# First and third attention: both heads of a pair multiplied at once in the two halves of the rows

## The reference, cut to what matters

```python
# A: 16 heads of 64, 4 key heads; a window of 3 blocks of 128 keys and all 256 context keys
s_loc = jnp.einsum('bqhgd,bkhd->bhgqk', qs, ks).astype(jnp.float32) * scale
s_ctx = jnp.einsum('bqhgd,bkhd->bhgqk', qs, kc).astype(jnp.float32) * scale
p = jax.nn.softmax(jnp.concatenate([s_loc, s_ctx, sink], axis=-1), axis=-1).astype(dt)
# and the 256 context queries against the 256 context keys, with the same heads
s = jnp.einsum('bqhgd,bkhd->bhgqk', qc, kc).astype(jnp.float32) * scale
# E: 8 heads of 64, 2 key heads; a chunk of 64 queries reads its own and 2 earlier chunks
s = jnp.einsum('bqhgd,bjhd->bhgqj', q_c, k_c).astype(F32) * scale
```

## Time and profile before

| | us |
|---|---|
| three runs | 2131.64, 2136.08, 2538.79 (median 2136.08) |
| the profiled execution | 2130.91 |
| its span | 2129.0 |
| PE busy in the span | 2009.5 (94%) |
| DVE busy | 997.8 (47%) |
| ACT busy | 882.3 (41%) |
| POOL busy | 698.8 (33%) |

### The profile page before, as it was taken

One profiled execution on the slowest core, in us unless ns is written; L12 is line 12 of the kernel. 1 busy time (PEld: TensorE's weight loads), 2 busy tenths in 40 slices (PEclk: granted clock), 3 DMA queues, 4 the chain that ended last, 5 costly groups with the idle time before them and its releaser, 6 DMA issues.

```text
span 2129.0 us, 28194 instructions
## 1 busy us (share of the span) xinstructions
PE 2009.5 (94%) x10600; PEld 1569.0 (74%) x10600; DVE 997.8 (47%) x1774; ACT 882.3 (41%) x1668; POOL 698.8 (33%) x394
## 2 busy tenths in 40 slices
PE   5999999999999999998899999999998899999998
PEld 3888655688665567887677888887885477888886
DVE  3520778523376653378436435343116625525254
ACT  4322667423376654535553222235225643323233
POOL 1322122342100045331234444443442334444433
PEclk9999999999999999998899999999999999999999
DMA  8222333132100013231124433332332122333332
GB/s 297 60 67 63 100 100 109 51 106 59 44 1 1 1 30 88 62 97 33 40 82 149 135 95 89 105 92 75 109 97 60 45 78 80 109 98 93 100 92 85
DMA packets 209467, 174.36 MB, mean 82 GB/s; under 512 B 6080, under 2 KB 180775, under 8 KB 208183
## 3 DMA queue, kind: packets, MB, share of 16 engines
q1 hardware_dynamic: 206096, 163.86, 25.4%
q0 software_dynamic: 2192, 8.45, 1.2%
q10 hardware_dynamic: 1047, 0.26, 0.1%
HBM read 170.41 MB, written 7.38 MB: 84 GB/s over the span
## 4 chain that ended last, share of the span: by engine, by line
PE 43%; issue 4%; ACT 2%; DVE 2%; POOL 2%; POOLq 0%; DVEq 0%; ACTq 0%
PE ps L369 13%; PE ps L371 13%; PE ps L370 13%; PE ps L737 1%; POOL WL L1563 1%; PE ps L701 1%; PE ps L599 1%; ACT PB L653 0%; ACT TMP L514 0%; PE ps L682 0%; DVE PB L641 0%; PE ps L618 0%; DVE XC L2549 0%; PE ps L448 0%; POOL YT L1551 0%
## 5 line engine op out<-in xcount | busy, mean ns | idle before, releaser
L1563 POOL TENSOR_TENSOR WL<-raww,WH 128x1024 fp32r<-128x1024 f32 (+1 forms) x247 | 583.2, 2366 | 910.1 <-ACT WH L321 901.1
L369 PE MATMUL ps<-HH,WH 128*128 128x512 f32 (+1 forms) x1368 | 523.2, 382 | 16.5 <-DVE HL L2529 7.8
L370 PE MATMUL ps<-HL,WH 128*128 128x512 f32 (+1 forms) x1368 | 519.1, 379 | 0.0
L371 PE MATMUL ps<-HH,WL 128*128 128x512 f32 (+1 forms) x1368 | 518.5, 379 | 0.0
L321 ACT ACTIVATE WH<-raww 128x1024 fp32r<-128x1024 f32 (+1 forms) x247 | 254.7, 1036 | 412.1 <-PE ps L371 408.8
L369 PEld LDWEIGHTS ps<-HH,WH 128*128 128x128 f32 x1368 | 259.6, 190 | 73.8 <-issue 17.8
L371 PEld LDWEIGHTS ps<-HH,WL 128*128 128x128 f32 x1368 | 259.6, 190 | 48.5
L370 PEld LDWEIGHTS ps<-HL,WH 128*128 128x128 f32 x1368 | 260.0, 190 | 46.7
L701 PE MATMUL ps<-ident,PB 128*128 128x128 f32 x952 | 157.5, 283 | 24.5 <-ACT PB L653 16.0
L653 ACT ACTIVATE PB<-PB,NB 128x512 f32<-128x512 f32 (+3 forms) x192 | 116.5, 607 | 72.7 <-DVE NB L641 69.8
L701 PEld LDWEIGHTS ps<-ident,PB 128*128 128x128 f32 x952 | 109.5, 142 | 50.2 <-ACT PB L653 26.9
(11 more groups left out here) (346 smaller groups left out, 3113.4 us busy)
## 6 DMA issues: line engine op xcount, KB each, us to landing
raww<-in_ffn_w_up SPq DMA_DIRECT2D x88, 512.0 KB, 3.8
raww<-in_ffn_w_down SPq DMA_DIRECT2D x40, 512.0 KB, 3.3
raww<-in_ada_w SPq DMA_DIRECT2D x32, 512.0 KB, 3.6
raww<-in_odd_w_in SPq DMA_DIRECT2D x24, 512.0 KB, 3.8
raww<-in_a_w_in SPq DMA_DIRECT2D x20, 512.0 KB, 3.8
raww<-in_even_w_in SPq DMA_DIRECT2D x17, 512.0 KB, 3.9
ADA<-in_ada_w SPq DMA_DIRECT2D x6, 1024.0 KB, 16.5
raww<-in_b_w_in SPq DMA_DIRECT2D x12, 512.0 KB, 3.8
```

Source lines behind the costliest of these rows:

```text
L369: nc.tensor.matmul(out, lh, rh, start=start and k == ks[0], stop=False)
L370: nc.tensor.matmul(out, lh, rl, start=False, stop=False)
L371: ins = nc.tensor.matmul(out, ll, rh, start=False, stop=stop and k == ks[-1])
L1563: nc.gpsimd.tensor_tensor(lo, raw_slot(k), hi.bitcast(F32), ALU.subtract).then_inc(*split_lo.mark(k))
```

## The change

A and E become paired as O is. For each `m` the order is now tile 0 of head 0, tile 0 of head 1, tile 1 of head 0, and so on, and `pair_scores` makes both tiles' scores in the even steps. It waits for the banks of both tiles before its first product. In E each tile has one bank of four (`single`); in A each has two, so a pair has all four. A tile's scores are three products of 64 rows instead of two of 128, and the two heads' products stand in turn. q high and q low of both heads are now made by one instruction each over all 128 rows (`both_q_high`, `both_q_low`), and earlier: in A in steps 2 and 3 of a block, and in E likewise. In the ctx tiles of A and in E, which of DVE and ACT copies the transposed probabilities alternates with i + hh instead of i. E uses other buffers for the probabilities (4 instead of 3), one of which shares memory with WL, so POOL waits for `pv_made["E", 5]` before it splits the weights that come next. For O only the helper's form changes.

```diff
         def pair_scores(pe, A, r, i):
-            w = A["jobs"][r]["tiles"][i]["n"] * P
+            if "score_wait" in A:
+                A["score_wait"](pe, r, i)
+            todo = []
             for h in (r, r + 1):
-                claim(pe, A["at"](h, i) % 4, (max_made, (A["name"], h, i)))
-            A["score_wait"](pe, r, i)
-            for n, (q, k) in enumerate(A["products"](r)):
-                for h in (r, r + 1):
-                    p0 = HD * (h % 2)
-                    ins = nc.tensor.matmul(ps[:, A["at"](h, i) % 4, 0:w], q[p0:p0 + HD, i * P:(i + 1) * P], k[p0:p0 + HD, 0:w],
-                                           start=(n == 0), stop=(n == 2), tile_position=(p0, 0))
-                    if n == 2:
-                        ins.then_inc(*scores_made.mark(A["name"], h, i))
+                t, tl = A["at"](h, i), A["jobs"][h]["tiles"][i]
+                first = t % 4 if A.get("single") else 2 * (t % 2)
+                spans = sorted({(tl["off"] + c0) // 512 for c0, _, _, _ in tl["parts"]})
+                for b in spans:
+                    claim(pe, first + b, (max_made, (A["name"], h, i)))
+                todo.append([(first + (tl["off"] + c0) // 512, (tl["off"] + c0) % 512, w, q, k) for c0, w, q, k in tl["parts"]])
+            for n in range(len(todo[0])):
+                for h in range(2):
+                    b, c, w, q, k = todo[h][n]
+                    same = [x for x in range(len(todo[h])) if todo[h][x][0] == b]
+                    ins = nc.tensor.matmul(ps[:, b, c:c + w], q, k, start=(n == same[0]), stop=(n == same[-1]),
+                                           skip_group_check=True, tile_position=(HD * h, 0))
+                    if n == len(todo[0]) - 1:
+                        ins.then_inc(*scores_made.mark(A["name"], r + h, i))
...
+        def both_q_high(act, A, m):
+            if m >= 2:
+                n = A["per"] * (m - 1) - 1
+                act.wait_ge(*scores_made[A["name"], n, A["jobs"][n]["nq"] - 1])
+            nc.scalar.activation(A["q2"][m % 2][:, 0, :], A["q"][:, m, :], ACT.Copy).then_inc(*act_out.mark("q2", A["name"], m))
+
+        def both_q_low(dve, A, m):
+            dve.wait_ge(*act_out["q2", A["name"], m])
+            nc.vector.tensor_tensor(A["q2"][m % 2][:, 1, :], A["q"][:, m, :], A["q2"][m % 2][:, 0, :].bitcast(F32),
+                                    ALU.subtract).then_inc(*dve_out.mark("q2", A["name"], m))
...
-                                q = a_q2[m % 2][:, hh, i * P:(i + 1) * P]
+                                qh, ql = (a_q2[m % 2][p0:p0 + HD, j, i * P:(i + 1) * P] for j in range(2))
                                 lo, hi = max(i - 1, 0), min(i + 2, NT)
                                 nl = hi - lo
-                                parts = [(0, C, q, k[:, S:R]) for k in (kh, kl)]
-                                parts += [(2 * P, nl * P, q, k[:, lo * P:hi * P]) for k in (kh, kl)]
+                                parts = [(c0, w, q, k[p0:p0 + HD, a:a + w]) for q, k in ((qh, kh), (ql, kh), (qh, kl))
+                                         for c0, w, a in ((0, C, S), (2 * P, nl * P, lo * P))]
...
-                                      "fill_pe": a_fill_pe, "fill_dve": a_fill_dve, "per": 4, "gate": a_gate,
+                                      "fill_pe": a_fill_pe, "fill_dve": a_fill_dve, "per": 4, "paired": True, "gate": a_gate,
...
-                                      "per": 2, "pt": lambda r: ((0, 1, 3)[(r + 1) % 3], 0), "bc": BC, "bc_free": lambda r: o_made["E", (r // 2, "lat")], "q": e_q, "k": e_k, "q2": e_q2, "kh": e_kh, "kl": e_kl}))
+                                      "per": 2, "paired": True, "single": True,
+                                      "pt": lambda r: ((4, 2, 5, 6)[r % 4], 0), "pt_free": lambda r: (r - 4) | 1, "bc": BC, "bc_free": lambda r: o_made["E", (r // 2, "lat")], "q": e_q, "k": e_k, "q2": e_q2, "kh": e_kh, "kl": e_kl}))
...
             split_low(pool, ("e_q", 3))
+            pool.wait_ge(*pv_made["E", 5])
             split_low(pool, ("o_q", 7))
```

More of the change, by code:

```diff
@@ L882, in finish_att @@
             if A.get("paired"):
-                A["seq"] = [(r + h, i) for r in range(0, len(jobs), 2) for i in range(NT) for h in range(2)]
+                A["seq"] = [(r + h, i) for r in range(0, len(jobs), 2) for i in range(jobs[r]["nq"]) for h in range(2)]
             else:
@@ L1007, in a_jobs @@
                             for i in range(2):
-                                q = a_q2[m % 2][:, hh, S + i * P:S + (i + 1) * P]
-                                tiles.append(tile(2, [(0, C, q, k[:, S:R]) for k in (kh, kl)], [(0, [4, 5], ("dve", "act")[i])],
+                                qh, ql = (a_q2[m % 2][p0:p0 + HD, j, S + i * P:S + (i + 1) * P] for j in range(2))
+                                tiles.append(tile(2, [(0, C, q, k[p0:p0 + HD, S:R]) for q, k in ((qh, kh), (ql, kh), (qh, kl))],
+                                                  [(0, [4, 5], ("dve", "act")[(i + hh) % 2])],
                                                   0, masks[:, 0:C]))
@@ L1324, in e_jobs @@
                     for i in range(NT):
-                        q = e_q2[m % 2][:, hh, i * P:(i + 1) * P]
                         lo = max(i - 1, 0)
                         nl = i + 1 - lo
-                        parts = [(0, nl * P, q, k[:, lo * P:(i + 1) * P]) for k in (e_kh[kv], e_kl[:, kv, :])]
-                        tiles.append(tile(nl, parts, [(0, list(range(lo, i + 1)), ("dve", "act")[i % 2])],
+                        qh, ql = (e_q2[m % 2][p0:p0 + HD, j, i * P:(i + 1) * P] for j in range(2))
+                        kh, kl = (k[p0:p0 + HD, lo * P:(i + 1) * P] for k in (e_kh[kv], e_kl[:, kv, :]))
+                        tiles.append(tile(nl, [(0, nl * P, q, k) for q, k in ((qh, kh), (ql, kh), (qh, kl))],
+                                          [(0, list(range(lo, i + 1)), ("dve", "act")[(i + hh) % 2])],
                                           0, masks[:, (7 - nl) * P:7 * P]))
@@ L1375, in o_jobs @@
                     w = (i + 1) * P
-                    tiles.append(tile(i + 1, None, [(0, list(range(i + 1)), ("dve", "act")[(i + m) % 2])],
+                    qh, ql, kh, kl = (b[m // 2 % 2][p0:p0 + HD, :] for b in (o_qh, o_ql, o_kh, o_kl))
+                    parts = [(0, w, q[:, i * P:(i + 1) * P], k[:, 0:w]) for q, k in ((qh, kh), (ql, kh), (qh, kl))]
+                    tiles.append(tile(i + 1, parts, [(0, list(range(i + 1)), ("dve", "act")[(i + m) % 2])],
                                       0, o_band[:, m % 4, 512 - w:512]))
```

69 lines of the change are left out of this document (27 added, 42 removed).

## The result

| | before | after |
|---|---|---|
| median of 14 runs, us | 2133.85 | 2138.65 |
| the profiled execution | 2130.91 | 2139.68 |
| A, between the linear products around it | 183.9 | 192.4 |
| E, likewise | 55.7 | 55.6 |
| O, likewise | 93.4 | 96.1 |

The ratio is 1.0027 with a 95% interval of 1.0019 to 1.0036: slower by 0.3%, under the 2% called slower here, but clear of noise. One of the 14 runs of before lies at 2538.79 and is left out of the ratio. The number (2138.65) is inside the range of 2113 to 2145; the sign is not the forecast one: I had 2129 against 2131.9 in my own sum (and 2136 as the median of the three runs then known).

What follows compares the result with a forecast made beforehand. PE, 94% busy, was taken to bound A before the change; in E engines wait for each other. The profiled 2130.9 + 4 (A) - 6.5 (E) + 1 (undisturbed runs) gave 2129 us, range 2113 to 2145.

Steps and rivals of the forecast that it cites:

- What the scores cost: PE in A: paired rounds 0.12 or 0.17 us apart, 17 us less issue time, 2 us returned by switches.
- The walk of a block and its multiplication: A: one block walked, 23.2 against 22.4 us; five blocks +0.9, three -0.3, plus 0.5 for waits: +4 us.
- My own sign: A: each pair's first score within 0.1 us of the second maximum's end in steps 2 to 8.
- the second failed step: E: 8 tiles in 9.2 us, by O's ratio 1.17; three pairs gain 2.0 each, the first 0.6: -6.5 us.
- the sign of being wrong that I had set: The forecast is wrong if A is under 176 us or E's tiles keep their 11 us.
- The sum: Whole kernel: 2130.9 + 4 for A - 6.5 for E + 1 for undisturbed runs = 2129 us.
- Rival 2: A's coupling costs more, each hand-over late, 0.35 us in each of 48 pairs: A +17, E -4, 2145; chance 0.17.
- Rival 1: PE's saved time in A comes through: A -9, E -8, whole 2115 us; chance 0.20.
- Rival 3: The clock falls in A, to 0.95: +4 or 5 us, 2134; chance 0.18 together with Rival 4.
- Rival 4: E gets no faster, bound by ACT's exponentials or the half clock: 2134 us; chance 0.18 together with Rival 3.
- my own case: Whole kernel: A +4 and E -6.5 us give 2129, own range 2122 to 2136; chance 0.42.
- Rival 5: The row halves don't overlap: 17 x 2 more us on PE, 2155; chance 0.03.

Runs made afterwards that it cites:

- swap_a: Changed kernel, but in A's step 2 ACT copies the spread out of its bank before making q high; A 191.2 us, median 2138.83, ratio 1.0028 to before.
- late_e: Changed kernel, but in E DVE's output work of an even step comes behind the pair's second maximum; E 48.7 us, median 2135.00, ratio 1.0008 to before.
- seq_a: Changed kernel, but in A a pair's score products are issued head after head instead of in turn; A 203.0 us, median 2150.68, ratio 1.0083 to before.
- late_a: Changed kernel, but in A DVE's even-step work other than maximum and copy comes behind the second maximum; A 192.1 us, median 2143.00, ratio 1.0040 to before.
- banks_a: Changed kernel, but A's tiles with 2 and 4 key blocks take one score bank each; A 187.5 us, median 2134.55, ratio 1.0010 to before.
- e_coupled: Changed kernel, but in E a pair's scores wait for both maxima of the pair before; E 56.5 us, median 2145.57, ratio 1.0062 to before.

## Why the prediction was wrong

1. **What the scores cost: right.** The rounds stand 0.12 and 0.17 apart, the groups of scores lost 14.7 us together (55.3 to 40.6), forecast 17 less 2 for the switches. That PE's saved time would then come through in steps 0, 1 and 4, 5 did not hold (item 2). The switches are in the records: from the last score to a transpose 0.21 instead of 0.12 (256 columns) and 0.27 instead of 0.18 (384); from a transpose to a score never under 0.20, where the old form had 0.03. That is 0.26 for in and out together, where I took 0.1 to 0.2 each. Behind a product with the values or a filler the scores start after 0.31 in both forms, so there the way in costs nothing more.
2. **The walk of a block and its multiplication: the kind right, the term short. First failed step.** A was forecast 4 us longer and got 8.5 longer. In the block that I walked each lat step is within 0.35 of the forecast, and it got 1.3 longer for 0.8. The loss where the maxima bind was sized well: 1.0 and 0.8 a block in steps 2, 3 and 6, 7 would be 14.4 in all, and 13.4 was measured. What failed is the rest:
   - The gains of the PE-bound steps did not come. The walk has 0.4 and 0.3 a block less in steps 0, 1 and 4, 5, which would be 5.6; measured was 0.6.
   - The hand-over from the second maximum to the next scores was put at 0.02 us and is 0.25 (319.04 to 319.29) ahead of steps 4 and 6 where the maximum binds, and 0.15 ahead of step 8. That is 0.6 of the 0.8 by which the walked block exceeds 22.9. My own sign, first scores within 0.1 of the maximum's end, was not met.
   - One block stood for all. The three that prepare keys (1, 3, 5) were to get 0.9 shorter together, from a length of 24.1 read in one of them, and got 1.5 longer: block 1 had lasted 23.0 (238.39 to 261.36) and lasted 24.3. Block 0 had lasted 18.5 and lasted 20.6, 1.2 of it in steps 0, 1 (1.83 to 3.00). The five others together got 6.2 longer for 4.5.
   - The first pair of the stage waits for all four banks, 0.8.

   Fillers in steps 2 and 3 are not among the missing parts, though swap_a gains 0.6 in three such steps: the old form had paid for them too (3.63 with one, 2.76 without, in the same steps). There are 32 fillers, not 28.
3. **E: the second failed step.** I took 1.17 of the fullest engine's work from O and put it on E, 2.0 us for each of three pairs of heads alike and 0.6 for the first. Nothing in E was walked. The first gained 1.6, the second 1.2, the third some 0.5 and the fourth nothing, 2.8 in the mean (56.8 of two profiles to 54.0 of nine), not 6.5; the third's 14.0 in the changed kernel is the sign of being wrong that I had set (tiles that keep their 11 us). In E three instructions of DVE, 1.8 us, stand between two maxima of a pair: the same pattern that I had priced in A, at three times its size, and late_e shows that they bind. With that order mended E gained 7 to 8 in all, near my 6.5, but not as I had it: the second and third pairs of heads take 10.2 and 10.5 for my 9.2, and 3 us come in the last eight tiles (20.7 to 17.4). That nearness is in part luck.
4. **The sum.** -6.5 became -2.8 and +4 became +8.5. From the median of the undisturbed runs of before (2133.49, where I had 2131.9) this gives 2139.2, and 2138.65 was measured. Two terms of opposite sign, each off by about 4 us in the same direction, turned a forecast of 2.5 less into 5 to 6 more; with either one alone put right the forecast would have been a small loss.
5. **The rivals.** Rival 2 (coupling costs more, E -4, 2145) was the nearest and had 0.17; it decides from a lat pair of 4.1 in the mean, and the four lat steps have 3.97. Its +17 is 0.35 for each of 48 pairs counted from before; on top of my own +4 it would be +21. Rival 1 fell: seq_a shows PE's time in the steps that it binds and none where the maxima do. Rival 3 did not occur in the changed kernel (A at 1.00), but did in late_a and seq_a. A mean of 0.95 between the two levels would be 18 us of A at 1.2 GHz, not 9. Rival 4 is nearer than my own case for E as changed, though E gained a little; E not faster at all would have been 2135.5 in my sum, not 2134. Rival 5 fell with the earlier trace rows and with seq_a, and its own 34 us would have given 2163, not 2155. The rule that I set beside rival 2 (the Trainium skill, Perfetto Trace Analysis, Matmuls: independent groups rotated through banks) agrees with banks_a (-4.9 in A) and e_coupled (+2.5 in E).

## What to carry to other kernels

When two tiles are made at once, whatever stands between their two first readers becomes part of the loop that frees their banks: list it, for every stage alike, and move the output, not the copies that free other banks. A walk through one block says little of a stage whose blocks differ: walk each kind, the first one and the ones with extra work too, and price the hand-over between engines from a row where one really waits for the other. And a stage should not be priced by another stage's ratio of time to work when the order within it can be read.

## What the runs showed of the hardware

- Row halves overlap even when the heads are issued one after the other: in seq_a twelve products of 256 columns, six of one half and then six of the other, took 1.25 us from the first to the next kind of product, where no overlap would give 0.22 + 11 x 0.12 + 0.21 = 1.75 and products in turn took 0.91. The second half's first product starts beside the third of the first half, and ahead of the first half's last two, which stand before it in the program.
- The granted clock rose from 0.72 to 0.98 in E with eight more small transposes a pair, and the stage's time stayed the same (54.2 for 53.2 to 55.6).
- In A, from the end of a maximum that binds to the start of the scores that waited for it 0.25 us pass (0.15 ahead of the first ctx scores), in the old form too (246.52, 248.31).
- Stage A, at the full clock, repeats to 0.1 us across kernels and chips, while the time ahead of it varied from 216.6 to 223.3: the difference of a stage says more in one profile than three rounds of the whole. That holds where the clock is 1.00; late_a's one profile, at 0.99, stood for its shortest execution.
